# Sparse-attention stage: TensorE takes the transpositions of two jobs in a row, then the value products, then the scores of the next two jobs

## What is computed

```python
# per head, for every query t; gt are sigmoid gates
ss = (q @ ks.T) * scale - slope * (t - kpos)      # keys of the selected blocks, causal
o_sel = softmax(ss) @ vs
sw = (q @ kw.T) * scale - slope * (t - kpos)      # keys of the last 512 positions, causal
o_win = softmax(sw) @ vw
o = gt[0] * o_cmp + gt[1] * o_sel + gt[2] * o_win
```

## Time and profile before

| | |
|---|---|
| runs | 3430.52, 3431.98, 3438.84 us, median 3431.98 us |
| the profiled execution | 3424.22 us, its span 3422.4 us |
| mean granted TensorE clock | 0.965 of full speed |
| TensorE busy | 3239.3 us (95%) |
| VectorE busy | 2012.8 us (59%) |
| ScalarE busy | 1170.8 us (34%) |
| the stage, first score product to the last value product | 847.36 to 1107.37 us |

### The profile page before, as it was taken

The page is one execution under the profiler, slowest core; times in us unless marked ns, Lnnn a source line. Parts: engine busy times, 40 slices in busy tenths (PEclk is TensorE's granted clock), DMA queues, the critical chain, the costliest instruction groups (busy, mean ns, idle before and its releaser), DMA issues. The chain is left out here.

```text
span 3422.4 us, 55938 instructions
## 1 busy us (share of the span) xinstructions
PE 3239.3 (95%) x22553; PEld 2682.3 (78%) x22553; DVE 2012.8 (59%) x3202; ACT 1170.8 (34%) x1980; POOL 884.7 (26%) x502
## 2 busy tenths in 40 slices
PE   8999999999999989999999899979888989999999
PEld 7878888877788777888888777758786768888887
DVE  5852666622886667777788434234434765555685
ACT  3112222112666223333345510344432053333443
POOL 2332333335310432222200233322221232222000
PEclk9999999999899999999999899979998989999999
DMA  4453344334000651343373274310012623333742
GB/s 129 142 189 121 112 123 120 113 110 141 25 9 12 226 166 59 93 124 104 113 256 122 72 204 115 113 64 22 21 40 79 206 86 106 95 93 123 252 136 96
DMA packets 355294, 387.95 MB, mean 113 GB/s; under 512 B 27328, under 2 KB 258290, under 8 KB 353834
## 3 DMA queue, kind: packets, MB, share of 16 engines
q1 hardware_dynamic: 327518, 303.89, 28.9%
q10 hardware_dynamic: 26560, 78.27, 6.0%
q0 software_dynamic: 960, 2.21, 0.3%
HBM read 271.98 MB, written 112.33 MB: 112 GB/s over the span
## 5 line engine op out<-in xcount | busy, mean ns | idle before, releaser
L1106 PE MATMUL bk<-ffn_bhi,ffn_ahi 128*128 128x512 f32 x1240 | 482.8, 394 | 25.8 <-DVE ffn_blo L1439 8.8
L1106 PE MATMUL bk<-ffn_blo,ffn_ahi 128*128 128x512 f32 x1240 | 480.6, 392 | 0.0
L1106 PE MATMUL bk<-ffn_bhi,ffn_alo 128*128 128x512 f32 x1240 | 480.3, 392 | 0.0
L223 PE MATMUL acc<-h_hi,whi 128*128 128x512 f32 x1136 | 373.2, 408 | 20.8 <-DVE h_lo L2757 6.0
L1072 POOL TENSOR_TENSOR ffn_alo<-ffn_raw,ffn_ahi 128x512 fp32r<-128x512 f32 x134 | 204.9, 1539 | 670.5 <-ACT ffn_ahi L1236 669.8
L223 PE MATMUL acc<-h_lo,whi 128*128 128x512 f32 x1136 | 357.3, 394 | 0.0
L223 PE MATMUL acc<-h_hi,wlo 128*128 128x512 f32 x1136 | 357.0, 393 | 0.0
L206 POOL TENSOR_TENSOR whi<-raw,ones 128x1024 fp32r<-128x1024 f32 (+1 forms) x83 | 159.8, 1925 | 749.0 <-PE acc L223 557.0
L1106 PEld LDWEIGHTS bk<-ffn_bhi,ffn_ahi 128*128 128x128 f32 x1240 | 234.9, 190 | 82.5 <-issue 28.8
L1106 PEld LDWEIGHTS bk<-ffn_blo,ffn_ahi 128*128 128x128 f32 x1240 | 235.2, 190 | 48.8
L1106 PEld LDWEIGHTS bk<-ffn_bhi,ffn_alo 128*128 128x128 f32 x1240 | 234.7, 189 | 49.4
(11 more groups left out here) (599 smaller groups left out, 6508.0 us busy)
## 6 DMA issues: line engine op xcount, KB each, us to landing
ffn_graw<-ffn_gated SPq DMA_DIRECT2D x154, 256.0 KB, 2.7
raw<-w_in SPq DMA_DIRECT2D x51, 512.0 KB, 4.0
projT<-proj_stage ACTq DMA_DIRECT2D x51, 512.0 KB, 2.9
mix_ada_raw<-w_ada SPq DMA_DIRECT2D x12, 2048.0 KB, 9.9
ffn_raw<-w_up SPq DMA_DIRECT2D x44, 512.0 KB, 5.0
ffn_gated<-ffn_gout SPq DMA_DIRECT2D x44, 512.0 KB, 3.2
ffn_gated<-ffn_gt SPq DMA_DIRECT2D x22, 768.0 KB, 6.2
ffn_drow<-w_down SPq DMA_DIRECT2D x44, 256.0 KB, 5.5
```

Of the source, the lines that this page charges most:

```text
L223: last = nc.tensor.matmul(acc[:, t, :], w[:, k, w_cols], x[:, k, t * HALF:(t + 1) * HALF], start=(k == 0 and i == 0), stop=(k == k_tiles - ...
L1106: ins = nc.tensor.matmul(o, wt[:, w, k, :], xt[:, x, k, :], start=first and i == 0, stop=last and i == 2, skip_group_check=reopened)
```

## The change

TensorE's own order in `nsa_attend` is written anew, and nothing else is changed. Job j+2's scores used to come before job j-1's transpositions, one job at a time; now each turn of the loop takes the transpositions of jobs 2m-1 and 2m, then the value products of double m-1, then the scores of both jobs of double m+1.

```diff
             scores(0)
             scores(1)
-            for j in range(NJ + 1):
-                if j + 2 < NJ:
-                    scores(j + 2)
-                if j > 0:
-                    turns(j - 1)
-                if j > 2 and j % 2 == 1:
-                    values((j - 3) // 2)
+            for m in range(NJ // 2):
+                if m > 0:
+                    turns(2 * m - 1)
+                turns(2 * m)
+                if m > 0:
+                    values(m - 1)
+                if 2 * m + 2 < NJ:
+                    scores(2 * m + 2)
+                    scores(2 * m + 3)
+            turns(NJ - 1)
             values(NJ // 2 - 1)
```

## The result

The changed kernel takes 3661.54 us, the median of 4 runs (3657.65 to 3670.4); the kernel before took 3431.25 us beside it. The ratio is 1.0671, 95% interval 1.0654 to 1.0688: slower by 6.7%, some 230 us. The forecast was 3640 us, between 3572 and 3700.

A forecast was written before the change was run, and what follows sets the result against it. The prediction took TensorE to bound the kernel, busy for 95% of the span. It summed 3424.2 + 150 (chain) + 60 (clock) = 3634 us for the profiled execution, 3642 for the median, stated as 3640; range 3572 to 3700.

The forecast's parts named there:

- TensorE sets the pace before, with VectorE nearly always in time: Old attention stage: TensorE busy 62.55 of 65.02 us per pair of heads, VectorE 52.37, nearly always done before TensorE asks.
- The closed chain: Attention stage: TensorE and VectorE wait for each other in turn, ScalarE's work between; +159 us at full clock.
- its rivals: Follow-up runs' alternatives: transpositions or scores in a row cost by themselves, or VectorE's or ScalarE's order is no link.
- 6.90 us for a turn of 5 tiles, and +159 us for the chain: Attention stage: a 5-tile double takes 6.90 us against 3.99 before; 64 doubles take 387 us against 228.
- the linear step: Attention stage: a double's time runs from 3.00 us at one tile by 0.975 per tile, 6.05 at the average 4.125.
- The +150 that I took instead: Chain term in the attention stage: taken as +150 us with bounds 135 to 165, instead of the summed +159.
- The clock, +60 us: Attention stage: TensorE's clock swings to 1.2 GHz in gaps, nearly half of 140 us; +60 us, bounds 0 to 140.
- My price for a slow double, 0.8 of its TensorE links: Doubles at 1.2 GHz: TensorE's chain links, 3.13 us at 5 tiles, take 1.8 times as long; 2.2 us a mean double.
- The 30 us of start, drain and slowed scalings kept in both: Old attention stage: some 30 us over its 228, including two falls of the clock, left in both kernels, nothing added.
- Nothing counted for fewer changes between kinds of product: TensorE in the attention stage: fewer score entries from a transposition would save 6 to 11 us if TensorE-bound; counted as nothing.
- The Trainium skill's rule on transpositions: TensorE's clock: transpositions don't count as activity as products do, putting the clock term nearer its upper end, 140 us.
- Waits of TensorE of 150 us or more, stage end near 1315, mean clock 0.7 to 0.85: Expected attention stage profile: TensorE waits ahead of even transpositions in nearly all 64 doubles; stage ends near 1315, not 1107.

The follow-up runs named there:

- scores between the turns: The changed kernel with both scores of double m+1 put between the transpositions of jobs 2m-1 and 2m; 3427.88 us, ratio 0.9996.
- The fill with products: The changed kernel with added matrix products that nothing reads ahead of each of the two transposition jobs; 3593.56 us, ratio 1.0477.
- the fill with transpositions: The changed kernel with two unread transpositions of the identity in place of each added unread product, at the same places; 3600.54 us, ratio 1.0493.

## Why the prediction was right, step by step

- *TensorE sets the pace before, with VectorE nearly always in time.* Shown: with the scores out in time (scores between the turns) the time of before is back, waits and all.
- *The closed chain.* Shown by the timeline, by the two-sided waits, and by edits that took out one link each, the values, VectorE's scaling and ScalarE's copies, and then the last two together. Each took time off, as the chain says and its rivals don't.
- *6.90 us for a turn of 5 tiles, and +159 us for the chain.* Measured 6.64 and 7.03 at full clock. The fill with products ran the last pair's doubles 4 to 14 at 1.00 throughout, in 74.38 us (1189.99 to 1264.37). Doubles 1 and 2 took 2.91 and 3.65 in the changed kernel at full clock (1222.33 to 1225.24 to 1228.89), and for double 3, which neither of the two has at full clock, I estimate 4.1, between its neighbours of 3.65 and 4.50. That is 85.0 us for fourteen doubles, 6.07 each, where the kernel before takes 3.57: 64 x 2.50 = 160 us. For two tiles the linear step gives 3.00 + 0.975 = 3.98, and 3.65 was measured, so single sizes were off, but the sum came out.
- *The +150 that I took instead.* This lowering had no ground in the rows, and the 159 was the better number.
- *The clock, +60 us, from "nearly half" of the stage at 1.2 GHz.* This term was sized somewhat too small. A mean clock of 0.71 means that (1 - 0.71) / 0.5 = 58% of the stage, 281 us, ran at 1.2 GHz. The fill with products brings this down to 85 us and the stage down by 59.6, which is at least 0.30 us for each us of slow clock. The changed kernel's own doubles say the same: fifteen of the doubles 2, 7, 8, 9, 13 and 15 that had a slow spell, each set beside the same double at full clock in another pair of heads, lost 24 us over 81 us of slow clock, 0.30 again. At this price the clock costs the changed stage 84 us, an estimate. The kernel before had 36 us of slow clock already, worth between nothing and half of that, so the added term is 66 to 84 where I put 60. My price for a slow double, 0.8 of its TensorE links, was wrong in both directions. Two tiles pay 4.49 - 3.65 = 0.84 us, where I had reckoned 0.8 x 1.76 = 1.4. The window double of tile 4 pays more than the 0.8 x 3.13 = 2.5 of a wholly slow double, though it is slow for only part of its time: 9.61 us in the last pair of heads against the 7.03 of the timeline above at full clock, so 2.6.

VectorE's even maxima of the changed kernel, for two tiles at full clock and at 1.2 GHz, and for that window double:

```profile
1113.45 0.42 DVE L3036 TENSOR_REDUCE att_small<-sc 128x1 f32<-128x256 f32 x1 [2.45 <-PE sc L2950]
...
1117.94 0.42 DVE L3036 TENSOR_REDUCE att_small<-sc 128x1 f32<-128x256 f32 x1 [2.24 <-PE sc L2950]
...
1225.24 0.42 DVE L3036 TENSOR_REDUCE att_small<-sc 128x1 f32<-128x256 f32 x1 [1.51 <-PE sc L2950]
...
1228.89 0.42 DVE L3036 TENSOR_REDUCE att_small<-sc 128x1 f32<-128x256 f32 x1 [1.40 <-PE sc L2950]
...
1266.77 0.82 DVE L3036 TENSOR_REDUCE att_small<-sc 128x1 f32<-128x640 f32 x1 [4.73 <-PE sc L2950]
...
1276.38 0.96 DVE L3036 TENSOR_REDUCE att_small<-sc 128x1 f32<-128x768 f32 x1 [6.62 <-PE sc L2950]
```

And the clock within that window double:

```profile
1268.00:1272.00 4.00, 2.14 (x12) 1.63 (x14) 1.73 (x4) 2.62 (x8) 0.00 (x0) 0.72 0.00 0
1272.00:1276.00 4.00, 4.00 (x28) 3.48 (x29) 0.00 (x0) 0.00 (x0) 0.00 (x0) 0.50 0.00 0
1276.00:1280.00 4.00, 2.08 (x13) 1.60 (x11) 3.52 (x8) 2.17 (x5) 0.00 (x0) 0.93 0.00 0
```

The slow spell lies on the burst, where VectorE and ScalarE have nothing to do, and full clock comes back for the gap, where TensorE has little to do. I had spread the slow share evenly over both. I had also expected the swing "in every larger double" and said nothing of the small ones; the doubles 1 to 3, of one and two tiles, ran at 0.50 throughout in three of the four pairs.

- *The 30 us of start, drain and slowed scalings kept in both.* Not tested alone, and it holds only in part: 160 for the chain and 66 to 84 for the clock make 226 to 244, and the stage grew by 224. So up to 20 us of what the old stage had over its 228 are gone; which, no run shows. Two terms that were too small and one that was too large cancel in part, and the closeness of the total, 210 against 224, owes something to that luck.
- *Nothing counted for fewer changes between kinds of product.* Scores between the turns has fewer of them than the kernel before as well, and is not faster by more than the interval: 0.9996 (0.998 to 1.0012), 7 us at most.
- *The Trainium skill's rule on transpositions* ("TensorE: Matmul & The Clock Gate", Part 4, PE-mode transpose), which I had weighed as a reason for the clock to stay down: the fill with transpositions held it at 0.90, as the products did. The measurement decides against it here, for transpositions that stand between bursts of products.
- *Waits of TensorE of 150 us or more, stage end near 1315, mean clock 0.7 to 0.85:* 121 us, 1336 and 0.71. The waits are a miss: half of the loss came as slower work of TensorE, 112 us, and not as waiting. Of the 21 us by which the stage ends later than 1315, 3.9 are its later start and 14 its length, 224 instead of 150 + 60. The two doubles of tile 4 took 6.64 to 9.61 us from maximum to maximum, where I had said 6.5 to 9.
- The measured median lies 21 us above the forecast. Execution against execution, the sum gave 3634 for the profiled one, and it took 3661.6: 14 of the 27 us are the stage's and 13 lie outside it, within what the rest of the program varies by from run to run. The 8 us that I had added from the profiled execution to the median hide part of this, since the median of the changed kernel (3661.54) lies on its profiled execution.

## What to carry to other kernels

In a loop over several in-order engines, ask for each wait what that engine has not yet issued behind it, and whether the awaited result needs it: grouping like with like on one engine removed the lookahead and made three engines take turns, and a double that took 4.1 us now takes 7.6 (260 and 484 us for 64). Put the work that feeds the other engines first and the work that only consumes last. When TensorE begins to wait, price its clock too: here it was 60 us or more of 230, and in the larger doubles the slow spells fell on the bursts.

## What the runs showed that I had not expected

- Unread TensorE work made a kernel faster by 61 to 68 us, as I expected before these runs but not in the prediction. It held the clock at 1.00, with one exception, in the doubles of three tiles and more; in the doubles 1 and 2 it stayed at 0.50, though TensorE was busy for 89% of the time (7.45 of 8.36 us).
- Unread transpositions did this as well as unread products: the mean clock of the stage rose from 0.71 to 0.90 with either, and the stage took 424.9 and 424.8 us.
- Moving the scores ahead of the values gave back 153 us, against 65 for the link itself at full clock by my sum. The clock rose with it, 0.71 to 0.90. At full clock in both runs the link measures 1.54 us a double over eight doubles of 5.1 tiles on average, against the 1.39 of my sum for 5 tiles. Scaled alike, that is some 70 us for 64 (an estimate), and the other half came with the clock.
